# A decoder layer with expert retrieval on one core: the first combine group by slices of the experts

## The reference

```python
def peer_ffn(h, w_q, sub_keys, u_experts, v_experts):
    ...
    g = jax.nn.softmax(best_s, axis=-1)
    def expert_chunk(args):
        xc, ic, gc = args
        act = jax.nn.gelu(jnp.einsum('cd,chkd->chk', xc, u_experts[ic]).astype(F32), approximate=False)
        wgt = (gc * act).astype(xc.dtype)
        return jnp.einsum('chk,chkd->cd', wgt, v_experts[ic])
...
    x = x + gate1 * mixed
    h2 = rmsnorm(x, g_norm2) * (1.0 + scale2) + shift2
    return x + gate2 * peer_ffn(h2, w_q, sub_keys, u_experts, v_experts)
```

## Time and profile before

| | us |
|---|---|
| runs of the kernel before, three | 2336.08, 2338.91, 2339.33 |
| median | 2338.91 |
| the profiled execution | 2338.76 |
| its span, first to last instruction | 2336.9 |
| TensorE busy in it | 2217.9 |
| VectorE, ScalarE, GpSimd busy | 1220.2, 779.7, 614.1 |
| the last matmul of the experts starts | 1611.28 |
| first matmul of the combine starts | 1627.39 |
| the last matmul starts | 2326.20 |

### The profile page before, as it was taken

One profiled execution on the slowest core, in us unless ns is written; L12 is line 12 of the kernel. 1 busy time (PEld: TensorE's weight loads), 2 busy tenths in 40 slices (PEclk: granted clock), 3 DMA queues, 4 the chain that ended last, 5 costly groups with the idle time before them and its releaser, 6 DMA issues. The chain is left out here.

```text
span 2336.9 us, 29988 instructions
## 1 busy us (share of the span) xinstructions
PE 2217.9 (95%) x11243; PEld 1833.1 (78%) x11243; DVE 1220.2 (52%) x1781; ACT 779.7 (33%) x912; POOL 614.1 (26%) x262
## 2 busy tenths in 40 slices
PE   5999789989889999999999999997999999999998
PEld 4888567777778788787788888886888888888886
DVE  6454465525566889942365656564343343344344
ACT  3222234433322222223345454544222222222221
POOL 0000670002300144444433333331232233232231
PEclk9999899999989999999999999998999999999999
DMA  7652233337614166555556666667656655655652
GB/s 273 234 198 72 76 89 94 95 107 230 190 26 104 36 144 149 139 135 135 140 166 199 192 185 180 190 192 253 204 170 213 207 173 195 215 182 177 211 175 81
DMA packets 291288, 375.21 MB, mean 161 GB/s; under 512 B 10858, under 2 KB 217499, under 8 KB 289180
## 3 DMA queue, kind: packets, MB, share of 16 engines
q1 hardware_dynamic: 291228, 374.44, 53.6%
HBM read 296.27 MB, written 77.60 MB: 160 GB/s over the span
## 5 line engine op out<-in xcount | busy, mean ns | idle before, releaser
L1471 POOL TENSOR_TENSOR u_lo<-u_ut,u_hi 128x1024 fp32r<-128x1024 f32 x127 | 313.0, 2465 | 485.3 <-ACT u_hi L1485 485.3
L117 PE MATMUL u_s<-h_hi,u_hi 128*128 128x512 f32 x1024 | 408.1, 399 | 8.9 <-DVE u_lo L1560 4.7
L117 PE MATMUL v_o<-v_v_hi,v_w_hi 128*128 128x512 f32 x1024 | 399.6, 390 | 15.7 <-DVE v_w_lo L1850 15.7
L119 PE MATMUL u_s<-h_hi,u_lo 128*128 128x512 f32 x1024 | 401.1, 392 | 0.0
L118 PE MATMUL u_s<-h_lo,u_hi 128*128 128x512 f32 x1024 | 400.3, 391 | 0.0
L119 PE MATMUL v_o<-v_v_hi,v_w_lo 128*128 128x512 f32 x1024 | 399.3, 390 | 0.0
L118 PE MATMUL v_o<-v_v_lo,v_w_hi 128*128 128x512 f32 x1024 | 399.3, 390 | 0.0
L1829 DVE TENSOR_TENSOR v_v_lo<-v_raw,v_v_hi 128x4096 fp32r<-128x4096 f32 x31 | 186.3, 6010 | 346.2 <-ACT v_v_hi L1809 346.2
L1539 DVE STREAM_TRANSPOSE u_ut<-u_raw 128x1024 f32<-128x1024 f32 x128 | 158.9, 1242 | 273.0 <-POOL u_lo L1471 266.8
L117 PEld LDWEIGHTS v_o<-v_v_hi,v_w_hi 128*128 128x128 f32 x1024 | 192.9, 188 | 56.3 <-issue 16.1
L117 PEld LDWEIGHTS u_s<-h_hi,u_hi 128*128 128x128 f32 x1024 | 193.5, 189 | 50.8 <-DVE u_lo L1560 4.9
(11 more groups left out here) (294 smaller groups left out, 3283.4 us busy)
## 6 DMA issues: line engine op xcount, KB each, us to landing
u_raw<-in_u_experts_dram SPq DMA_DIRECT2D x256, 256.0 KB, 5.4
v_raw<-in_v_experts_dram SPq DMA_DIRECT2D x32, 2048.0 KB, 7.9
expert_acts<-u_ao SPq DMA_DIRECT2D x64, 512.0 KB, 3.2
expert_gates<-u_gs SPq DMA_DIRECT2D x16, 2048.0 KB, 6.4
v_gt<-expert_gates SPq DMA_DIRECT2D x32, 1024.0 KB, 13.1
w_in_raw<-in_w_in_dram SPq DMA_DIRECT2D x17, 1024.0 KB, 5.6
proj_ada<-in_w_ada_dram SPq DMA_DIRECT2D x8, 2048.0 KB, 8.3
gate_w_raw<-in_w_in_dram SPq DMA_DIRECT2D x32, 512.0 KB, 4.1
```

Of the source, the lines that this page charges most:

```text
L117: nc.tensor.matmul(out, w[0], x[0], start=first, stop=False)
L119: return nc.tensor.matmul(out, w[1], x[0], start=False, stop=last)
L1471: nc.gpsimd.tensor_tensor(lo[j][:, :, :], ut[j][:, :, :], hi[j][:, :, :].bitcast(F32), ALU.subtract).then_inc(sem["lo_ok"], 1)
```

## The change

Three things. TensorE's first group is `opening` and no longer `group(0, 0, True)`: the four slices are the outer loop and the eight banks the inner one, and slice x waits for its own halves only (a new semaphore `lo0_ok`). VectorE and ScalarE do values and weights of group 0 in turn, slice by slice (with a new semaphore `wh0_ok` for the high halves of the weights). And since the program needs two semaphores more, GpSimd clears those of the first phase while `phase_query` runs, so that they can be given out again.

```diff
@@ -348,6 +348,8 @@
                 pe.wait_ge(h_ok, 4 * i - 4)
                 pe.wait_ge(hv_ok, 4 * i - 4)
                 transposes(i)
+
+        return range(rows_in.num, acc_c.sem.num + 1)
 
 
 def phase_project(nc, a, keep, xt, space, raw, w_in, hi_ok, lo_ok):
@@ -1217,7 +1219,7 @@
     largest(nc, [scores[:, i, x, :] for i, x in at], [top[:, i, x, :] for i, x in at], [topi[:, i, x, :] for i, x in at], step, fence)
 
 
-def phase_query(nc, a, keep, scores, top, topi, ranked, raw, w_in, ahead):
+def phase_query(nc, a, keep, scores, top, topi, ranked, raw, w_in, ahead, spent):
 
     with ExitStack() as stack:
         k = Kit(nc, stack, "query", X2_AT + 16 * KB)
@@ -1244,6 +1246,10 @@
                 for j in range(2):
                     sp.wait_ge(sem["lo_ok"], 2 * i + j)
                     load_queries(sp, a, raw[j], w_in[j], 2 * i + j)
+
+        @block.gpsimd
+        def _(pool):
+            nc.gpsimd.sem_clear(spent)
 
         @block.scalar
         def _(act):
@@ -1747,7 +1753,7 @@
         sq = k.sb("sq", [P, D])
         assert k.at <= V_AT
         p_o = [k.ps(f"o{i}", [P, D]) for i in range(TT)]
-        names = ("w_in1 w0_ok hi0_ok gf_in vhi_ok vlo_ok w_ok whi_ok wlo_ok mm "
+        names = ("w_in1 w0_ok hi0_ok wh0_ok lo0_ok gf_in vhi_ok vlo_ok w_ok whi_ok wlo_ok mm "
                  "ssq_ok root_ok y_ok out_ok").split()
         sem = {n: k.sem(n) for n in names}
         dve_c = k.count("dve_chain")
@@ -1798,8 +1804,11 @@
         @block.scalar
         def _(act):
             act.wait_ge(sem["v_in"], 16)
-            for x in range(GT):
+            def first(x):
                 nc.scalar.activation(v_hi[0][:, x, :], v[:, x, :], ACT.Copy).then_inc(sem["hi0_ok"] if x < GT - 1 else sem["vhi_ok"], 1)
+
+            first(0)
+            first(1)
 
             def split(g, j, first=False):
 
@@ -1812,7 +1821,9 @@
 
             for x in range(GT):
                 act.wait_ge(sem["w0_ok"], x + 1)
-                nc.scalar.activation(w_hi[0][:, x, :], at[0][:, x, :], ACT.Copy).then_inc(sem["hi0_ok"] if x < GT - 1 else sem["whi_ok"], 1)
+                nc.scalar.activation(w_hi[0][:, x, :], at[0][:, x, :], ACT.Copy).then_inc(sem["wh0_ok"] if x < GT - 1 else sem["whi_ok"], 1)
+                if x + 2 < GT:
+                    first(x + 2)
             split(1, 1, True)
             with act.Fori(1, NG // 2) as i:
                 for j in range(2):
@@ -1830,25 +1841,26 @@
                 dve.wait_ge(sem["whi_ok"], g + 1)
                 nc.vector.tensor_tensor(w_lo[j][:, :, :], at[j][:, :, :], w_hi[j][:, :, :].bitcast(F32), ALU.subtract).then_inc(sem["wlo_ok"], 1)
 
-            for x in range(GT):
-                if x < GT - 1:
-                    dve.wait_ge(sem["hi0_ok"], x + 1)
-                else:
-                    dve.wait_ge(sem["vhi_ok"], 1)
-                ins = nc.vector.tensor_tensor(v_lo[0][:, x, :], v[:, x, :], v_hi[0][:, x, :].bitcast(F32), ALU.subtract)
-            ins.then_inc(sem["vlo_ok"], 1)
-            dve.wait_ge(sem["w_in0"], 32)
             for x in range(GT + 1):
                 if x < GT:
+                    if x < GT - 1:
+                        dve.wait_ge(sem["hi0_ok"], x + 1)
+                    else:
+                        dve.wait_ge(sem["vhi_ok"], 1)
+                    ins = nc.vector.tensor_tensor(v_lo[0][:, x, :], v[:, x, :], v_hi[0][:, x, :].bitcast(F32), ALU.subtract)
+                    if x == GT - 1:
+                        ins.then_inc(sem["vlo_ok"], 1)
+                    if x == 0:
+                        dve.wait_ge(sem["w_in0"], 32)
                     o = at[0][:, x, :].rearrange("p (c t) -> p c t", t=CH)
                     nc.vector.tensor_tensor(o, o, gt[0][:, :, x * CH:(x + 1) * CH], ALU.mult).then_inc(sem["w0_ok"], 1)
                 if x:
                     if x < GT:
-                        dve.wait_ge(sem["hi0_ok"], GT - 1 + x)
+                        dve.wait_ge(sem["wh0_ok"], x)
                     else:
                         dve.wait_ge(sem["whi_ok"], 1)
                     ins = nc.vector.tensor_tensor(w_lo[0][:, x - 1, :], at[0][:, x - 1, :], w_hi[0][:, x - 1, :].bitcast(F32), ALU.subtract)
-            ins.then_inc(sem["wlo_ok"], 1)
+                    ins.then_inc(sem["lo0_ok"] if x < GT else sem["wlo_ok"], 1)
             split(1, 1)
             with dve.Fori(1, NG // 2) as i:
                 split(2 * i, 0)
@@ -1877,6 +1889,20 @@
 
         @block.tensor
         def _(pe):
+            def opening():
+                for x in range(GT):
+                    if x < GT - 1:
+                        pe.wait_ge(sem["lo0_ok"], x + 1)
+                    else:
+                        pe.wait_ge(sem["vlo_ok"], 1)
+                        pe.wait_ge(sem["wlo_ok"], 1)
+                    for n in range(8):
+                        ts, cs = slice(n // 2 * P, (n // 2 + 1) * P), slice(n % 2 * S, (n % 2 + 1) * S)
+                        ins = three(nc, p_o[n // 2][:, cs], (w_hi[0][:, x, ts], w_lo[0][:, x, ts]), (v_hi[0][:, x, cs], v_lo[0][:, x, cs]),
+                                    x == 0, False)
+                        if x == GT - 1:
+                            ins.then_inc(sem["mm"], 1)
+
             def group(g, j, first=False, last=False):
                 pe.wait_ge(sem["vlo_ok"], g + 1)
                 pe.wait_ge(sem["wlo_ok"], g + 1)
@@ -1887,7 +1913,7 @@
                                     first and x == 0, last and x == GT - 1)
                     ins.then_inc(sem["mm"], 1)
 
-            group(0, 0, True)
+            opening()
             group(1, 1)
             with pe.Fori(1, NG // 2 - 1) as i:
                 for j in range(2):
@@ -1910,7 +1936,7 @@
         w_hi_ok, w_lo_ok = kw.sem("hi_ok"), kw.sem("lo_ok")
         ky = Kit(nc, top, "y", Y_AT)
         y_hi, y_lo = (ky.sb(n, [P, NBR * CB, S], F32R) for n in ("hi", "lo"))
-        phase_condition(nc, a, keep, w_raw, w_in, y_hi, w_hi_ok, w_lo_ok)
+        spent = phase_condition(nc, a, keep, w_raw, w_in, y_hi, w_hi_ok, w_lo_ok)
         if stop <= 1:
             return
         xt = Kit(nc, top, "mixin", XT_AT).sb("xt", [P, 2 * MIX_BLOCKS, S])
@@ -1954,7 +1980,7 @@
         best_keys = kt.sb("top", [P, TT, 2 * PH, TOPK]), kt.sb("topi", [P, TT, 2 * PH, TOPK], U32)
         assert kt.at <= V_AT
         ranked = kt.count("ranked")
-        phase_query(nc, a, keep, scores, *best_keys, ranked, q_raw, q_in, first_experts)
+        phase_query(nc, a, keep, scores, *best_keys, ranked, q_raw, q_in, first_experts, spent)
         if stop <= 6:
             return
         acts = nc.dram_tensor("expert_acts", [NE // P, P, S], F32, kind="Internal").ap()
```

## The result

| | kernel before | the change |
|---|---|---|
| median of 22 runs, us | 2338.09 (2335.01 to 2339.33) | 2341.06 (2339.01 to 2342.86) |
| ratio, with 95% interval | | 1.0016, 1.0009 to 1.0022 |
| span of the profiled execution, us | 2336.9 | 2339.8 |

The interval, less one, times 2338.09 is 2.1 to 5.1 us; the medians differ by 3.0 us, and the ratio gives 3.7 us. The change is slower by 0.13% by the medians and 0.16% by the ratio: a small loss, but one whose interval leaves out no difference. With 22 runs of each kernel the interval reaches 0.07% to either side, so less than the prediction's 0.2% can be told from no change.

A forecast was written before the change was run, and what follows sets the result against it. The prediction took the combine to be bound by TensorE, through its matmul groups' starts and the clock. Group 1's later start, +1.39, plus the clock's fall, +2.1, gave +3.5 us on 2338.8: 2342.3 us, range 2338.0 to 2345.0.

The forecast's parts named there:

- TensorE's start: First matmul of group 0: needing slice 0 only, it would come at 1625.15, 2.24 us earlier.
- transfers of group 1: SyncE's queue: values 3 of group 0 end 6.93 us later, so all 4 MB of group 1 come that much later.
- group 1 starts later by: First matmul of group 1 on TensorE: at 1653.26 against 1651.87, that is 1.39 us later.
- the wait before it: TensorE between group 0 and group 1: a new idle stretch of 3.63 us.
- half speed after it: TensorE's clock after the new wait: falls to half, costing 2.1 us, with ends 1.7 and 2.7.
- wait after group 1: Group 2 on TensorE: weights ready about 1668.8, needed at 1677, so no wait there or later.
- the 2.07 us of the earlier trace: Idle stretch in the kernel before's trace, followed by 3.4 us at half speed, worth 1.7 us; a basis for the clock term.
- the opening's own slow stretch: Slow clock at the combine's first matmuls, worth 2.7 us; taken as present before and after, so cancelling.
- the case without a fall of the clock: Rival: after TensorE's new wait the clock stays up, only +1.39 us, 2340.2 us; 12 in 100.
- The case without lateness: Rival: group 1's transfers take 3.6 us less, TensorE doesn't wait and keeps the 2.24 us, 2336.5 us; 8 in 100.
- The slower one: Rival: group 1's values transfer takes 9.7 us, not 7.8, making the chain 1.9 us later; 2344.2 to 2344.8 us; 14 in 100.
- the case of the banks: Rival: three matmuls per bank keep group 0 at half speed, costing 16.6 us, group 1 14.4 us late, 2353 us; 4 in 100.

The follow-up runs named there:

- late_8: Kernel before plus the semaphores' clearing, SyncE issuing group 1's transfers only after the sixth matmul of group 0; ratio 1.0017 against the kernel before.
- late_11: Kernel before, with SyncE waiting for TensorE's first bank of group 0 before issuing group 1's transfers; ratio 1.0039 against the kernel before.
- change_2: The change run again unaltered, on one chip beside a version with 16 more matmuls in group 0; ratio 1.0015 against the kernel before.
- banks_only: Kernel before with only TensorE's first group reordered, slices outside and banks inside, after the same wait for all of group 0; ratio 0.9999.
- weights_ahead: The change, with group 1's activations and gates issued before SyncE's wait for the values' low half; ratio 0.9988 against the kernel before.

## Why the prediction was right

Every date is counted from the issue of group 0's gates, at 1615.80 before and 1615.70 after.

| step | predicted | measured |
|---|---|---|
| TensorE's start earlier by | 2.24 | 11.59 - 9.10 = 2.49 |
| transfers of group 1 later by | 6.93 | 12.55 - 5.77 = 6.78 |
| group 1 starts later by | 1.39 | 37.33 - 36.07 = 1.26 |
| the wait before it | 3.63 | 3.57 |
| half speed after it | 3 to 5 us, cost 2.1 (1.7 to 2.7) | 3.4 us, cost 1.7 |
| sum | +3.5 | +2.95 in the trace, +3.0 by medians, +3.7 by the ratio |
| wait after group 1 | none | none |

- *TensorE's start.* Right. The quarter of a microsecond over is the gates, which landed 6.02 us after their issue and not 6.17, and 0.05 us from the last weights to TensorE instead of 0.15.
- *The transfers.* Right as a rigid shift. GpSimd's part moved with it:

```profile
1642.71 5.90 POOL L1795 TENSOR_TENSOR v_at<-v_at,v_gt 128x2048 f32<-128x2048 f32 x1 [40.87 <-DMA v_gt<-expert_gates]
```

GpSimd starts 27.01 us behind the gates where the earlier trace rows had 20.08, 6.93 us later.
- *The clock.* The mechanism was right and the size a little high: the lower end of the range I had given, 1.7, is what happened in the profiled execution, as after the 2.07 us of the earlier trace rows. The choice of 2.1 was between two rows; in late_8 and late_11 it was 2.9 us. The statement that the opening's own slow stretch cancels was too simple. In the kernel before a longer one makes the whole program longer. In the change group 1 starts when its data are there, so a shorter one only makes the wait longer: in change_2 it was 4.5 us instead of 5.6, half of which is 0.6, and the wait 4.35 instead of 3.57.
- *Group 2.* Right that there was no wait. Its weights were ready at 1669.07, predicted 1668.8, but the closeness is luck: the gates landed at 1658.49 and not near 1659.8, and GpSimd's multiplication took 6.30 us and not 4.6, with VectorE on the values until 1660.33.
- *The level.* 2342.3 was 1.2 us above the measured median. Of this 0.5 us is the sum, and 0.7 us the level: the profiled execution and the median of three runs that it was built on lay above the median of 22 (2338.09).
- *What the time alone would say.* Little. The range, 7 us wide, takes in 2338.09 too, that is, no change at all; and the measured 2341.06 lies nearer to the 2340.2 of the case without a fall of the clock than to 2342.3. It is the dates in the trace, and the kernels above, that bear out the mechanism.
- *The rivals.* The case without lateness, the case without a fall of the clock and the case of the banks didn't happen, the last shown wrong by banks_only. The slower one didn't either: the values of group 1 landed 1636.05 - 1628.25 = 7.80 us after their issue, as before.

## What to carry to other kernels

Before an instruction is put in front of another, ask what its neighbours' ends release: here the last of four cheap instructions freed a buffer, and the next group's four megabytes waited for it. Starting a bound engine early is worth only as much as the slack of its second portion allows; past it the gain turns into an idle stretch, and on TensorE such a stretch of 3.6 us and more cost another 1.6 to 2.9 us here, through the clock. If work can be done while a transfer is awaited (the three value slices under the gates' transfer), keep it there, and change only the order on the engine that gains from it.

## What the runs showed of the hardware

- A wait of 3.6 to 5.8 us in front of group 1 brought TensorE's clock to half for 3.4 us in two executions (waits of 3.57 and 4.35) and for 6.8 us in two (4.44 and 5.83), of which the last 5.8 us were work and the first 1 us the end of the wait; waits of 0.56 us and less didn't. The 2.07 us of the earlier trace rows also had 3.4 us behind them. In late_8 the wait was 0.09 us longer than in change_2, and the slow stretch twice as long.
- GpSimd's and VectorE's instructions on two tensors don't run beside each other. GpSimd's multiplication takes 4.62 us alone. In the change it started at 1642.71 while VectorE was on the values until 1644.14, and ended at 1648.61, 4.47 us after VectorE; before it ended 4.48 us after. In weights_ahead it is recorded from 1628.10 to 1634.11, over a run of VectorE's instructions; those that started up to 1628.95 took no longer than usual, and the last, from 1629.7, took 4.92 us and ended at 1634.65, 0.54 us after GpSimd's. The Trainium skill ("SBUF — State Buffer", "SBUF: two separate sides") says that the two share a pair of ports, which the first to come keeps for its whole instruction. The trace agrees that one stands while the other works; that the first to come goes first it doesn't show, for GpSimd's instruction, recorded first, didn't delay two of VectorE's that started behind it.
- SyncE stood 9 us on the issue of one 512 KB row behind 4 MB of other transfers (9.02 us before, 9.12 in the change), and 0.51 us on the same issue in weights_ahead, where only the 2 MB of values had been issued just in front of it. What the amount in front must be for this no run varied.
